# Conditioning sums by block transposes, first loads reordered, and chunks taken in pairs in a two-block network on one core

## The reference, cut to what matters

```python
mod = silu(c) @ w_ada + b_ada                 # 2048 -> 6 * 2048; again with c_2, twice 3 * 2048
sh1, sc1, ga1, sh2, sc2, ga2 = split(mod, 6)
h = rms_norm(x, g_norm1) * (1 + sc1) + sh1
... = split(h @ w_in)                         # mLSTM in both directions, neighbourhood attention
x = x + ga1 * (concat(h_a, h_b) @ w_out)
h = rms_norm(x, g_norm2) * (1 + sc2) + sh2
x = x + ga2 * conv_glu(h, w_up, conv_w, conv_b, w_down)
x = rms_norm(x, g_final)
# second block: a gated spatial mixer (sgu), then latent attention (mla), each as
h = rms_norm(x, pre_g[i]) * (1 + scale) + shift
x = x + gate * rms_norm(mixer(h), post_g[i])
```

## Time and profile before

| what | us |
|---|---|
| median of 3 runs | 2559.79 (2558.49 to 2563.99) |
| the profiled execution's own time | 2558.37 |
| its span | 2556.6 |
| TensorE busy in the span | 2389.7 |
| VectorE busy | 1980.4 |
| ScalarE busy | 1118.8 |

### The profile page before, as it was taken

The page is one execution under the profiler, slowest core; times in us unless marked ns, Lnnn a source line. Parts: engine busy times, 40 slices in busy tenths (PEclk is TensorE's granted clock), DMA queues, the critical chain, the costliest instruction groups (busy, mean ns, idle before and its releaser), DMA issues.

```text
span 2556.6 us, 33044 instructions
## 1 busy us (share of the span) xinstructions
PE 2389.7 (93%) x13438; PEld 2077.7 (81%) x13438; DVE 1980.4 (77%) x2463; ACT 1118.8 (44%) x1376; POOL 11.3 (0%) x12
## 2 busy tenths in 40 slices
PE   1499999998999999999997999999999997999996
PEld 1488887886888888888886888888888885888985
DVE  7988898798888777777787878677777676675765
ACT  1143344544454433444444434544444333455542
POOL 0000000000000000000000000000000000000000
PEclk9999999999999999999998999999999998999998
DMA  8979766685777688666684888766777773664342
GB/s 333 360 272 339 250 226 229 211 299 204 262 260 258 227 284 283 231 239 241 230 267 159 308 310 298 258 225 225 259 254 262 263 273 107 240 214 148 131 166 99
DMA packets 118297, 620.13 MB, mean 243 GB/s; under 512 B 13313, under 2 KB 14465, under 8 KB 75393
## 3 DMA queue, kind: packets, MB, share of 16 engines
q1 hardware_dynamic: 69840, 446.19, 49.7%
q10 hardware_dynamic: 48304, 171.82, 18.6%
HBM read 615.86 MB, written 2.10 MB: 242 GB/s over the span
## 4 chain that ended last, share of the span: by engine, by line
PE 87%; DVE 9%; issue 2%; ACT 1%; DMA 1%; POOL 0%; POOLq 0%; SPq 0%; ACTq 0%; DVEq 0%
PE pm L511 30%; PE ps L511 15%; PE pm L512 15%; PE ps L512 8%; PE pm L552 2%; PE pm L554 2%; PE pm L553 2%; DVE acc_first L1346 2%; PE pv L488 1%; DVE w_lo L1290 1%; PE ps L552 1%; PE ps L554 1%; PE ps L553 1%; DVE nt L1375 1%; DVE h L1381 1%
## 5 line engine op out<-in xcount | busy, mean ns | idle before, releaser
L1290 DVE TENSOR_TENSOR w_lo<-raw,w_hi 128x2048 fp32r<-128x2048 f32 (+2 forms) x412 | 892.1, 2165 | 327.0 <-ACT w_hi L896 326.1
L511 PE MATMUL pm<-h,w_hi 128*128 128x512 f32 x2526 | 896.8, 399 | 22.1 <-DVE h L1381 18.3
L896 ACT ACTIVATE w_hi<-raw 128x2048 fp32r<-128x2048 f32 (+2 forms) x412 | 746.3, 1812 | 387.3 <-DMA raw<-in_w_down 136.7
L512 PE MATMUL pm<-h,w_lo 128*128 128x256 f32 x2526 | 706.0, 280 | 0.0
L511 PEld LDWEIGHTS pm<-h,w_hi 128*128 128x128 f32 x2526 | 476.6, 189 | 139.0 <-issue 19.6
L512 PEld LDWEIGHTS pm<-h,w_lo 128*128 128x128 f32 x2526 | 478.4, 189 | 0.2
L511 PE MATMUL ps<-h,w_hi 128*128 128x512 f32 x1314 | 464.3, 396 | 0.0
L1305 DVE SCALAR_TENSOR_TENSOR acc<-ada,csil,acc 128x512 f32<-128x512 f32 x600 | 449.7, 749 | 13.4
L512 PE MATMUL ps<-h,w_lo 128*128 128x256 f32 x1314 | 366.0, 279 | 0.0
L511 PEld LDWEIGHTS ps<-h,w_hi 128*128 128x128 f32 x1314 | 246.5, 188 | 59.7 <-issue 2.2
L512 PEld LDWEIGHTS ps<-h,w_lo 128*128 128x128 f32 x1314 | 247.3, 188 | 0.1
(11 more groups left out here) (365 smaller groups left out, 2901.1 us busy)
## 6 DMA issues: line engine op xcount, KB each, us to landing
ada<-in_ada ACTq DMA_DIRECT2D x320, 512.0 KB, 5.4
raw<-in_w_up SPq DMA_DIRECT2D x88, 1024.0 KB, 4.9
raw<-in_w_in SPq DMA_DIRECT2D x56, 1024.0 KB, 6.3
raw<-in_w_down SPq DMA_DIRECT2D x64, 704.0 KB, 5.5
raw<-in_sgu_v SPq DMA_DIRECT2D x32, 1024.0 KB, 5.1
raw<-in_sgu_u SPq DMA_DIRECT2D x32, 1024.0 KB, 5.1
raw<-in_sgu_z SPq DMA_DIRECT2D x32, 1024.0 KB, 4.9
raw<-in_sgu_out SPq DMA_DIRECT2D x32, 1024.0 KB, 4.9
```

Source lines behind the costliest of these rows:

```text
L511: pe.matmul(dst[:, :], wh[:, k, :], hl, start=(kc == 0), stop=False, skip_group_check=True)
L512: mm = pe.matmul(dst[:, 0:T], wl[:, k, :], hi, start=False, stop=last, skip_group_check=True)
L896: act.activation(w_hi[:, q % HSLOTS, 0:n], raw[:, q % SLOTS, 0:n], ACT.Copy).then_inc(hi_ready, 1)
L1290: tt_(w_lo[:, q % SLOTS, 0:n], raw[:, q % SLOTS, 0:n], whole(w_hi[:, q % HSLOTS, 0:n]), ALU.subtract).then_inc(lo_ready, 1)
```

## The change

1. SP: `par`, then the conditioning pieces; the gate weights after the first unit, x and `ident` after the second, `mask_a` and a new constant `sel` (0.11 MB) behind all eight.
2. First norm: ACT squares into four buffers, TensorE sums each pair over the partitions directly, behind the sums of the third unit; VectorE does no adds. Root and reciprocal come in the sixth unit, `gw_lo` in the second.
3. `split(0)` stands ahead of the norm on ACT and VectorE, on VectorE behind the last unit's products and ahead of its `take`; `split(1)` ahead of the norm on ACT, behind it on VectorE.
4. ACT: the gates' Exp and Ln stand behind the first `begin`, so behind `split(2)`, and ahead of the copy of `ka`'s first column.
5. Units 8 to 47: VectorE transposes `acc` in blocks of 32 x 32 into the buffer of the last piece, and adds up each row of 32; 16 numbers per partition stay in `fold`. Seven times TensorE sums a group of one or two vectors (4 or 8 units) with four products with slices of `sel`, and VectorE takes them with their bias. The 40 sums with ones and 40 takes are gone.
6. ADA_SPANS: `ka` 24 pieces over pieces 2 to 15 (26 over 16 before), `vb` 17 (16), `w_out` 21 (20).
7. Norms 2 to 5: the last pair of squares is not added by VectorE but given to TensorE; the sums lie in the bank `px[0]`.
8. The first two columns of `w_up0` and `lat` are a `column_pair`; `sgu_v`'s first block waits for each tile by itself.

```diff
-ADA_SPANS = [("ka", 0, 16, 26), ("va", 0, 8, 14), ("qb", 0, 16, 20), ("vb", 0, 15, 16), ("w_out", 0, 13, 20),
+ADA_SPANS = [("ka", 2, 14, 24), ("va", 0, 8, 14), ("qb", 0, 16, 20), ("vb", 0, 15, 17), ("w_out", 0, 13, 21),
+FOLDS = [(GA1, 1), (SH2, 2), (GA2, 1), (S0, 2), (G0, 1), (S1, 2), (G1, 1)]
...
             sp.dma_start(par[:, :], a["par"]).then_inc(const_in, 16)
-            sp.dma_start(ident[:, :], a["ident"]).then_inc(const_in, 16)
-            sp.dma_start(flat(x[:, :, :]), a["x"]).then_inc(x_in, 16)
-            sp.dma_start(flat(gw[:, :, :]), a["gate_w"]).then_inc(mix_const_in, 16)
-            sp.dma_start(flat(mask_a[:, :, :]), a["mask_a"]).then_inc(mix_const_in, 16)
             for u in range(FIRST_UNITS):
+                if u == 1:
+                    sp.dma_start(flat(gw[:, :, :]), a["gate_w"]).then_inc(mix_const_in, 16)
+                if u == 2:
+                    sp.dma_start(flat(x[:, :, :]), a["x"]).then_inc(x_in, 16)
+                    sp.dma_start(ident[:, :], a["ident"]).then_inc(ident_in, 16)
...
+            sp.dma_start(flat(mask_a[:, :, :]), a["mask_a"]).then_inc(mask_in, 16)
+            sp.dma_start(sel[:, :], a["sel"]).then_inc(sel_in, 16)
...
+            def fold_group(n):
+                v, count = FOLDS[n]
...
+                pe.wait_ge(ada_used, (v + count) * UNITS * APIECES)
+                s = v * UNITS % FOLD_UNITS
+                src = fold[:, s:s + count * UNITS, :].rearrange("p u (c j) -> p (u c) j", j=P // BLOCK)
+                for j in range(P // BLOCK):
+                    lo = P - BLOCK - BLOCK * j
+                    mm = pe.matmul(pv[:, 0:count * KC], sel[:, lo:lo + P], src[:, :, j], start=(j == 0), stop=(j == 3))
...
+                for j in range(2):
+                    pe.matmul(pn[:, half * T:(half + 1) * T], ones[:, :], total[:, j, :], start=(j == 0), stop=False)
+                if half:
+                    pe.wait_ge(sqg_ready, PAIRS)
+                else:
+                    pe.wait_ge(sq_ready, SQUARED[name])
+                for j in range(2):
+                    mm = pe.matmul(pn[:, half * T:(half + 1) * T], ones[:, :], last[:, j, :], start=False, stop=(j == 1))
...
-            sum_squares("norm1")
-            for u in range(FIRST_UNITS):
+            for u in range(3):
                 sum_first(u)
+            for p in range(PAIRS):
+                pe.wait_ge(x_sq, p + 1)
+                for j in range(2):
+                    mm = pe.matmul(pn[:, 0:T], ones[:, :], pre_bufs[p % 4][:, j, :], start=(p + j == 0), stop=(p + j == PAIRS))
...
             def add_ada(p):
...
+                if k == APIECES - 1:
+                    chain.link(ins)
+                    turned = ada[:, p % ASLOTS, 0:UCOLS]
+                    chain.link(dve.transpose(turned, acc[:, :]))
+                    ins = dve.tensor_reduce(fold[:, u % FOLD_UNITS, :], turned.rearrange("p (j b) -> p j b", b=BLOCK), AX.X, ALU.add)
                 ins.then_inc(ada_used, 1)
...
-            add_squares("norm2", PAIRS - 1)
+            take_group(1)
+            modulation("norm2", "g2", 0, SC2)
             rsqrt_mean("norm2", D)
-            modulation("norm2", "g2", 0, SC2)
```

More of the change, by code:

```diff
@@ L121 @@
 PAIRS = KC // 2
-NORMS = ["norm1", "norm2", "final", "post0", "post1"]
-ADDED = {n: PAIRS * (i + 1) for i, n in enumerate(NORMS)}
+NORMS = ["norm2", "final", "post0", "post1"]
+ADDED = {n: (PAIRS - 1) * (i + 1) for i, n in enumerate(NORMS)}
+SQUARED = {n: PAIRS * (i + 1) for i, n in enumerate(NORMS)}
 SUMS = {n: i + 1 for i, n in enumerate(["norm1", "norm2", "final", "finalg", "post0", "pre1", "kv", "q", "post1"])}
@@ L176, in build @@
         ada = sb("ada", [P, ASLOTS, APIECE])
-        acc = sb("acc", [P, 2, UCOLS])
+        acc = sb("acc", [P, UCOLS])
+        fold = sb("fold", [P, FOLD_UNITS, UCOLS // BLOCK])
+        sel = sb("sel", [P, 2 * P - BLOCK])
         par = sb("par", [P, NPAR])
@@ L550, in tokens @@
                             kc = 4 * part + k
+                            if need is not None and tt == 0:
+                                need(kc)
                             h_hi, h_lo = h[:, kc, tt * P:(tt + 1) * P], h[:, kc, T + tt * P:T + (tt + 1) * P]
@@ L697, in w_in_after @@
                 if (part, j) in B_WAVES:
+                    if B_WAVES[part, j] == 0:
+                        fold_group(0)
                     b_wave(B_WAVES[part, j])
@@ L952, in _, with gate_logs @@
             act.dma_start(flat(bias_b[:, :, :]), a["bias_b"]).then_inc(bias_in, 16)
-            for q in range(AHEAD):
-                split(q)
-            act.wait_ge(gate_rows, 1)
-            chain.link(act.activation(gates[0:GROW, 3, :], gates[0:GROW, 2, :], ACT.Exp))
-            act.activation(gates[0:GROW, 3, :], gates[0:GROW, 3, :], ACT.Ln, bias=1.0).then_inc(gate_exp, 1)
+            def gate_logs():
+                act.wait_ge(gate_rows, 1)
+                chain.link(act.activation(gates[0:GROW, 3, :], gates[0:GROW, 2, :], ACT.Exp))
+                act.activation(gates[0:GROW, 3, :], gates[0:GROW, 3, :], ACT.Ln, bias=1.0).then_inc(gate_exp, 1)
             def a_head_scores(hd_):
@@ L1324, in begin @@
                     urgent()
-                for u in TAKE_AT.get(q, ()):
-                    take(u)
                 for p in ADA_AT.get(q, ()):
@@ L1407, in _ @@
                     take(u - 1)
+                if u == 1:
+                    dve.wait_ge(gw_hi_ready, 1)
+                    tt_(gw_lo[:, :, :], gw[:, :, :], whole(gw_hi[:, :, :]), ALU.subtract).then_inc(gw_lo_ready, 1)
+                if u == 5:
+                    rsqrt_mean("norm1", D)
+            split(0)
             take(FIRST_UNITS - 1)
@@ L1410, in _ @@
             normed("norm1", SH1)
-            for q in range(AHEAD):
-                split(q)
+            split(1)
             G = slice(0, GROW)
@@ L1822, in constants @@
         cst[m % ROPE, 1024 + m] = 1.0
-    return {"ident": np.eye(P, dtype=f), "mask_a": mask_a.reshape(P, -1), "wmask": np.concatenate([win, win]), "mla_cst": cst}
+    sel = np.zeros((P, 2 * P - BLOCK), f)
+    sel[np.arange(P), P - BLOCK + np.arange(P) % BLOCK] = 1.0
+    return {"ident": np.eye(P, dtype=f), "sel": sel, "mask_a": mask_a.reshape(P, -1), "wmask": np.concatenate([win, win]), "mla_cst": cst}
 def blocks(w, k=KC):
```

127 lines of the change are left out of this document (77 added, 50 removed).

## The result

| | before | after | ratio |
|---|---|---|---|
| median of the runs, us | 2559.14 (2558.39 to 2563.99) | 2514.49 (2513.22 to 2519.61) | 0.9825 [0.9807, 0.9844] |
| profiled execution: own time, span | 2558.37, 2556.6 | 2513.22, 2511.2 | |

What follows compares the result with a forecast made beforehand. TensorE, busy 93%, was taken as the bound after the start, VectorE's conditioning pieces and DMA before. 12.2 + 4.0 + 29.6 + 13.7 - 3 - 1 = 55.5 us gave a median of 2504; range 2492 to 2519 us.

Steps and rivals of the forecast that it cites:

- the likeliest case: The forecast itself, given chance 0.62: whole kernel at 2498 to 2511 us.
- The start: Conditioning pieces loaded first, first split ahead of the norm: first column of weights at 117.1 us, 12.2 us earlier.
- 96.4: End of the 64 conditioning pieces on VectorE at the start, 4.6 + 82.1 + 1.7 + 5.3 + 2.7 us, against 108.6 before.
- rival (b): Start saves little: x landing in over 7 us holds up the sums, 4 of 12.2 us left, 2512; chance 0.08.
- Gate logarithm: ACT's Exp and Ln behind the third split, so low halves come sooner in the first part: 4.0 us gained.
- Unit sums: 40 unit sums leave TensorE, 32.0 us, less 2.4 for groups: 29.6 net, before 4 us of losses through VectorE.
- The 1 us foreseen in the `w_down` stages: Three folds in each w_down stage, where a piece lasts only 3.85 us, now and then delay TensorE: 1 us lost.
- no stall: First 16 pieces: VectorE busy 88.5 of some 92 us, so no loss; other stages have a fifth of VectorE free.
- rival (a): VectorE becomes the bound in the first stages and w_out; loses 12 to 15 us, 2517; chance 0.17.
- `w_out`: Extra piece and folds on VectorE exceed its lead of about 4 us, so TensorE waits: 3 us lost (0 to 5).
- The norms: Last squares summed without VectorE's add, paired columns at norm2 and lat, earlier sums at final: 13.7 us gained together.
- third low half decides: At norm2 and lat, the late third low half limits what pairing the first two columns gains to 3.6 us each.

Runs made afterwards that it cites:

- oldsums: Changed kernel with TensorE's 40 unit sums and their 40 takes back, no transposes, folds or groups; 2537.37 us, 0.9912.
- nofold: Changed kernel with one 16-column copy in place of transpose and reduction, conditioning vectors of units 8 to 47 not computed; 2505.35 us, 0.978.
- spans2: Changed kernel with conditioning pieces moved: 6 over pieces 4 to 7 of vb, 12 over first 6 of oa, 20 over 15 slots of w_out; 2510.27 us, 0.9804.
- nopair: Changed kernel with w_up0 and lat begun column after column, waiting for four tiles of h at a time; 2520.52 us, 0.9843.
- again: The changed kernel, unedited, in another execution; 2513.94 us, 0.9812.
- again2: The changed kernel, unedited, once more, on the same chip as spans2b; 2516.34 us, 0.9821.
- blip1: Changed kernel with one product of one column where each of the 40 unit sums used to stand; 2516.03 us, 0.9823.
- oldstart: Changed kernel with the old start order: SP queue, root and gate weights ahead of the units, first two splits behind the norm; 2523.25 us, 0.9858.
- spans: Changed kernel with conditioning pieces moved: 7 in first 7 of vb, 14 in the 8 of oa, 17 in 15 slots of w_out; 2512.34 us, 0.9809.
- spans2b: The kernel of spans2 run again, beside the unedited changed kernel on the same chip; 2509.55 us, 0.9801.

## Why the prediction was right, and where it was not

Faster was right, and 2514.5 lies in the range of 2492 to 2519, but above the 2498 to 2511 of the likeliest case: the sum was 10 us too good. Some of the agreement is luck: two errors in the unit sums went opposite ways, and a cost that nobody forecast (the pace) happened to leave the total inside the range. Step by step, with what was measured in its place:

**The start: 12.2 us forecast, 10.5 in the profile.** The mechanism held. Of the steps of "96.4", the first product came 1.0 us late (its piece landed only then) and the second piece another 1.2 us late; the inserts took 1.65 and 5.7 us (1.7 and 5.3 forecast), the low part of the gate weights ran inside the second gap as forecast (1.55 us at 29.05), and the root cost its 2.7. That makes 99.0; the last product ended at 99.3. The first split ran at 101.61 and not 98.6, since its raw piece only landed at 99.6 (96.7 forecast), and the last take stood behind it, so the norm began at 104.22. From there to the first column it was 14.5 us, 15.0 forecast. (In the other two profiles that column starts at 118.9 and 117.7.) By rival (b), x landing in over 7 us would spoil the gain: it took 14.7 us (the DMA issues), and did no harm, because the root was not due before 76.16.

**Gate logarithm: 4.0 us forecast, about 4.4 read.** `ka` went from 50.87 to 44.72 us; `oldsums`, which keeps the unit sums, needed 46.48, and 50.87 - 46.48 = 4.39. No run moves the logarithm alone, so this term is read from stage lengths and not isolated.

**Unit sums: 25.6 us forecast, 22.5 to 23.8 measured.** 29.6 us net were forecast for TensorE, with 4 lost through VectorE. `oldsums` gives the net, and `nofold` puts VectorE's loss at 8.6, twice the 4; so TensorE's side is 31 to 32 us, a little above its forecast. The two misses cancel in part: TensorE gained some 2 us more than forecast, VectorE cost 4.6 us more. The 1 us foreseen in the `w_down` stages is not seen: with the pace taken out, `w_down0` takes 123.0 us in the changed kernel and 122.9 in `nofold`, `w_down1` 137.0 in both.

**The step that failed: "no stall" in the stages before `w_out`.** I looked at the busy share of the first 16 pieces and of `w_out`, and took "all others have a fifth of VectorE free" as cover. In `kb` and `vb` that fifth is not free at the moment at which it matters. VectorE's list is in a fixed order, and the two folds in `kb` (at 322.12 and 366.90) stand ahead of the output of head 3, on which TensorE and then ACT's `vb` wait, while TensorE, freed of its own sums, comes sooner. VectorE entered `vb` with a lead of 1.2 us where it had 4.9 (3.6 in `nofold`, so 2.4 of the 3.7 us are the folds; 6.3 in `oldsums`, which has neither the folds nor the sooner TensorE). It was 3 us late at the head, and `vb` became 3.4 us longer than before; it is 61.0 in `nofold` and 60.7 in `oldsums`, as before. Another 3.6 us were lost there before the change too, and `spans2` gains them by taking the two pieces away from ahead of the head (57.3). Already before, TensorE waited 2.0 us at this place; the trace of before showed it, and the prediction never priced it. This was rival (a)'s mechanism in a stage that neither it nor the forecast named.

**`w_out`: 3 us forecast, 3.9 measured.** The stage took 103.8 us against 99.9 in `nofold`. TensorE's waits on low halves there are only 2.3 us; they vanish in `nofold`. Low halves are ready 4.2 us ahead at the third column, as the forecast's "one column's slack" has it, and 0.1 us at the eighth.

**The norms: 13.7 us forecast, 12.4 measured** in the changed kernel's profile, from the end of the last product ahead of the norm to the start of the third piece behind it: `norm2` 26.7 to 23.0, `final` 33.0 to 29.2, `lat` with `post0` 44.6 to 40.4, the end of the kernel 23.1 to 22.4. Of the pairs, "third low half decides" held: in `nopair` the two transitions take 26.3 and 43.9, so they bring 3.3 and 3.5 us, 3.6 each forecast. What the forecast left out is the lead that they use up, and with it about 1 us in `w_up0`. At `final`, TensorE and VectorE of the changed kernel, beside the earlier trace rows:

```profile
1345.85 0.98 PE L512 MATMUL pv<-fold,sel 128*128 128x32 f32 x8
...
1349.05 0.89 ACT L1124 ACTIVATE sqtg<-x,par 128x256 f32<-128x256 f32 x2
...
1351.02 1.03 PE L608 MATMUL px<-sqtg,ones 128*128 128x256 f32 x4
1352.16 0.42 DVE L1423 TENSOR_SCALAR rstd<-px 128x256 f32<-128x256 f32 x1 [3.17 <-PE px L608]
```

From ACT's last squares to the root it is 3.11 us now (1352.16 - 1349.05), 6.16 before (1383.10 - 1376.94): 3.05 of the 3.0 forecast. In `again` it was less: the granted clock was 0.50 from 1349.8 to 1353.2, so these sums took 2.07, 1.79 and 1.03 us, and `final` ended some 1.8 us later than in the other two profiles.

**Not in the forecast at all: the pace of the columns.** In the 290 columns that every kernel makes one at a time there are 4798 steps from one pair of products to the next. What they take beyond 346.8 ns a step (each column's mean from the starts of TensorE's records, cut at 354.5 ns so that waits stay out) is the pace's share; the span less that share compares programs better than one span does:

| us | before | after | `again` | `again2` | `blip1` | `nofold` | `oldsums` | `oldstart` | `nopair` | `spans` | `spans2` | `spans2b` |
|---|---|---|---|---|---|---|---|---|---|---|---|---|
| span | 2556.6 | 2511.2 | 2512.2 | 2516.1 | 2514.2 | 2504.6 | 2533.9 | 2524.2 | 2518.9 | 2509.8 | 2508.7 | 2505.9 |
| pace's share | 16.0 | 22.1 | 19.6 | 25.8 | 20.9 | 24.8 | 19.3 | 26.6 | 22.0 | 20.9 | 26.8 | 22.2 |
| rest | 2540.6 | 2489.1 | 2492.6 | 2490.3 | 2493.3 | 2479.8 | 2514.6 | 2497.6 | 2497.0 | 2488.9 | 2481.9 | 2483.6 |

By the rest, the change brings 49.9 us (2540.6 less the mean of its three, 2490.7), the second new spread 7.9 more, the sums' part 23.9, the order of the start 6.9 and the pairs 6.3, while the folds cost 10.9. The measured terms, 10.5 + 4.4 + 23.9 + 12.4 = 51.2 us, agree with the 49.9 within the 3.5 us by which the rests of the three profiles of one program differ. So of the 10.3 us that the profiled pair lacks to the forecast (55.5 less 45.2), 6.1 are pace and about 4.3 the terms above.

Part of the slow pace goes with the change. In `sgu_u` and `sgu_out` its share is 1.5 and 2.0 us before and 1.6 and 2.0 in `oldsums`, the two kernels with unit sums, and 3.3 to 3.4 and 3.1 to 3.4 us in every other profile but one (1.9 in `sgu_u` of `spans2b`): some 3 us that seem to go with the unit sums. Why the sums matter was not found; `blip1`'s small products do not have their effect. In `w_up0` the pace's share rose from 1.0 us to between 3.1 and 4.2, and 1.7 to 2.5 us of waits came in, so the stage got longer although its four unit sums left it.

## What to carry to other kernels

A free fifth of an engine covers new work only where its list has slack at the next hand-over: before work is added to an engine, go through the waits that already end on it or on one that it feeds, and price each as if it came later by the added work. What counts is the lead at that place, which all work since the last slack has used up, and not only the work just ahead of it. Where work can be put at several stages, put it behind the last hand-over of a stage, not ahead of it; moving 11 pieces out of `vb` here brought 4 to 7 us. Look at the next hand-over as well: `spans` lost 3.9 us at the start of `w_out` and `spans2` 3.1 us at `norm2` to the work that they had moved there. And before a few microseconds are put down to an edit, profile the unedited kernel twice.

## What the runs showed of the hardware that was not expected

At a granted clock of 1.00 and with no waits, the same pair of products (512 and 256 columns) repeats at one of a few distances, 346.5 to 346.7 ns, 350.0 or 353.3 ns in the mean, and keeps it for most or all of a stage. It can differ between executions of one program: `w_up1` took 244.1 us (43 of 44 columns at 346.7) in two of the three profiles of the changed kernel and 248.7 (44 of 44 at 353.3) in the third, `sgu_z` 181.0, 177.6 and 181.0. Over the kernel this makes 19.6 to 25.8 us, 6 us between profiles of one program. It depends on the program as well: 38 columns ran at 350.0 in the kernel before and 38 in `oldsums`, and none in any kernel without unit sums. What selects the pace is open; small products between columns (`blip1`) did not, and the chip was not held fixed.

In `vb` the granted clock was 0.55 from 409.0 to 412.8, after waits of 0.55, 1.07 and 2.39 us in the 12 us before; in `nofold` it was 0.52 from 405.0 to 408.5, around the end of a single wait of 2.06 us, and in `spans2`, without such waits, 1.00 all through the stage. In `again` it was 0.50 from 401.0 to 404.0, after waits of 0.70 and 1.07 us alone, with products between and behind them. So waits as short as these can cost the clock, and which of them does differed between executions.

At `final` TensorE did two products (four records) of each sum in 1.03 us at a granted clock of 1.00, where before it needed 2.08 us at 0.50, after 5.11 us of idle time. The fold's products and another sum stood just ahead of it, but they did not secure the clock: in `again` the same products stood there, and the next sum took 2.07 us.
